# Summing layer 1's modulation on VectorE inside the value-table stage, instead of on GpSimd

## The reference

```python
mod = silu(c) @ ada_w[l] + ada_b[l]            # ada_w[l]: 1024 x 6144
sh1, sc1, g1, sh2, sc2, g2 = split(mod, 6)     # shifts, scales, gates of the layer
...
a = einsum('td,thkd->thk', tc, u_tab[ec])      # first expert table, 16384 x 1024
w = gate * gelu(a)
y = einsum('thk,thkd->td', w, v_tab[ec])       # second expert table, 16384 x 1024
```

## Time and profile before

| | |
|---|---|
| median of 3 runs | 2510.07 us (2504.06 to 2512.12) |
| the profiled execution: time | 2507.17 us |
| its span, first to last instruction | 2505.2 us |
| mean granted TensorE clock | 0.943 |
| PE matmul busy | 2200.2 us (88%) |
| DVE busy | 1557.7 us (62%) |
| ACT busy | 1188.2 us (47%) |
| POOL busy | 1122.4 us (45%) |
| DMA, mean over the span | 151 GB/s |

### The profile page before, as it was taken

The page is one execution under the profiler, slowest core; times in us unless marked ns, Lnnn a source line. Parts: engine busy times, 40 slices in busy tenths (PEclk is TensorE's granted clock), DMA queues, the critical chain, the costliest instruction groups (busy, mean ns, idle before and its releaser), DMA issues.

```text
span 2505.2 us, 40525 instructions
## 1 busy us (share of the span) xinstructions
PE 2200.2 (88%) x13500; PEld 1974.4 (79%) x13500; DVE 1557.7 (62%) x2323; ACT 1188.2 (47%) x2096; POOL 1122.4 (45%) x472
## 2 busy tenths in 40 slices
PE   5897789999997588988998968799999965999998
PEld 4786679999997567767776857799999955788886
DVE  7578338994003978888975862599900069555555
ACT  8521434555545753433442232445555467455553
POOL 0003036988887545556550300578888865000000
PEclk9698789999998999999998987899999989999999
DMA  7632033555553025665563311345555510455553
GB/s 261 223 110 84 37 136 136 181 183 185 179 182 126 0 89 199 226 209 216 211 224 129 127 59 59 130 155 178 184 184 184 177 58 0 141 193 193 193 193 109
DMA packets 103453, 378.55 MB, mean 151 GB/s; under 512 B 11488, under 2 KB 11872, under 8 KB 102880
## 3 DMA queue, kind: packets, MB, share of 16 engines
q1 hardware_dynamic: 102672, 373.74, 42.9%
q10 hardware_dynamic: 720, 4.00, 0.4%
HBM read 375.46 MB, written 2.23 MB: 151 GB/s over the span
## 4 chain that ended last, share of the span: by engine, by line
PE 33%; issue 24%; POOL 24%; DVE 12%; DMA 3%; ACT 2%; POOLq 1%; DVEq 0%; SPq 0%; ACTq 0%
PE bank L1586 21%; POOL split_lo L472 19%; PE bank L1564 3%; PE bank L1286 3%; POOL hots L483 3%; DMA ring<-stream 2%; PE bank L1249 1%; POOL ada_acc L499 1%; DVE hots L1142 1%; DVE w_lo L1175 1%; POOL ada_ring L497 1%; DMA ada_ring<-stream 1%; DVE split_lo L1174 1%; DVE hots L1140 1%; PE bank L1460 1%
## 5 line engine op out<-in xcount | busy, mean ns | idle before, releaser
L472 POOL TENSOR_TENSOR split_lo<-ring,split_hi 128x1024 fp32r<-128x1024 f32 x296 | 728.7, 2486 | 247.2 <-ACT split_hi L689 246.9
L1497 PE MATMUL bank<-h_hi,split_hi 128*128 128x256 f32 x2304 | 657.1, 285 | 29.7 <-DVE h_lo L1084 21.3
L1499 PE MATMUL bank<-h_hi,split_lo 128*128 128x256 f32 x2304 | 654.6, 284 | 0.0
L1498 PE MATMUL bank<-h_lo,split_hi 128*128 128x256 f32 x2304 | 654.6, 284 | 0.0
L1174 DVE TENSOR_TENSOR split_lo<-ring,split_hi 128x1024 fp32r<-128x1024 f32 x248 | 381.2, 1537 | 229.0 <-ACT w_hi L765 228.9
L1497 PEld LDWEIGHTS bank<-h_hi,split_hi 128*128 128x128 f32 x2304 | 444.6, 193 | 34.7 <-issue 18.6
L764 ACT ACTIVATE split_hi<-ring 128x1024 fp32r<-128x1024 f32 x248 | 263.2, 1061 | 428.1 <-PE bank L1586 356.2
L1498 PEld LDWEIGHTS bank<-h_lo,split_hi 128*128 128x128 f32 x2304 | 444.8, 193 | 0.0
L1499 PEld LDWEIGHTS bank<-h_hi,split_lo 128*128 128x128 f32 x2304 | 444.8, 193 | 0.0
L689 ACT ACTIVATE split_hi<-ring 128x1024 fp32r<-128x1024 f32 x296 | 298.5, 1051 | 274.0 <-PE bank L1499 273.8
L1586 PE MATMUL bank<-split_hi,w_hi 128*128 128x512 f32 x1024 | 326.0, 400 | 21.4 <-DVE w_lo L1175 21.3
(11 more groups left out here) (271 smaller groups left out, 2791.9 us busy)
## 6 DMA issues: line engine op xcount, KB each, us to landing
ring<-stream SPq DMA_DIRECT2D x658, 512.0 KB, 3.2
ada_ring<-stream SPq DMA_DIRECT2D x48, 512.0 KB, 4.7
spill<-tables ACTq DMA_DIRECT2D x1, 1152.0 KB, 4.2
tables<-spill ACTq DMA_DIRECT2D x1, 1152.0 KB, 7.2
xT<-x_in SPq DMA_DIRECT2D x1, 1024.0 KB, 10.0
s5raw<-s5w ACTq DMA_DIRECT2D x2, 512.0 KB, 5.1
y_out<-hT SPq DMA_DIRECT2D x1, 1024.0 KB, 3.9
KM<-mixc SPq DMA_DIRECT2D x1, 576.0 KB, 8.0
```

Source lines behind the costliest of these rows:

```text
L472: gp.tensor_tensor(split_lo[:, j, :], ring[:, (e0 + j) % RING, :], split_hi[:, j, :].bitcast(F32), ALU.subtract)\
L1497: mm(dst, hi, x_hi, start=start, stop=False, skip_group_check=not group)
L1498: mm(dst, hi, x_lo, start=False, stop=False, skip_group_check=not group)
L1499: return mm(dst, lo, x_hi, start=False, stop=stop, skip_group_check=not group)
```

## The change

The `ada_w` blocks of layer 1 are summed by DVE. The GpSimd loop is removed. DVE's loop over the value stage of layer 0 becomes six rounds of 20 blocks (and 8 blocks singly, of which the first four of the stage stand ahead of the loop as before), with one operation for each `ada_w` block, two turns after SP has issued its transfer. SP's turns become 0, 2, 4, 6, 9, 11, 13, 15. PE's code is the same. DVE's loop for layer 1 is the same as before.

```diff
+ADA_TURNS = (0, 2, 4, 6, 9, 11, 13, 15)
...
-                ada_turns = (0, 1, 4, 6, 8, 10, 12, 14)
                 with sp.Fori(0, ADA // KT, 1) as i:
                     for j in range(20):
                         sp.wait_ge(v_ready, i * 20 + (l * KEYS + SPLIT + j + 1))
                         fetch(i * 20 + (late + RING + j), (late + RING + j) % RING)
-                        if j in ada_turns:
-                            k = ada_turns.index(j)
+                        if j in ADA_TURNS:
+                            k = ADA_TURNS.index(j)
                             sp.wait_ge(ada_used, i * 8 + (ADA + k - 1))
...
-                    with pool.Fori(0, ADA // KT, 1) as i:
-                        for k in range(KT):
-                            pool.wait_ge(ada_filled[k % 2], i * (16 * KT // 2) + 16 * (k // 2 + 1))
-                            silu = siluc[:, k:k + 1].broadcast_to([P, BLOCK])
-                            if k == 0:
-
-                                pool.wait_ge(ada_columns, i + ADA // KT)
-                                gp.tensor_tensor(ada_acc[:, :], ada_ring[:, 0, :], silu, ALU.mult).then_inc(ada_used, 1)
-                            else:
-                                b = ada_ring[:, k % 2, :]
-                                gp.tensor_tensor(b, b, silu, ALU.mult).then_inc(ada_scaled, 1)
-                                pool.wait_ge(ada_scaled, i * (KT - 1) + k)
-                                gp.tensor_tensor(ada_acc[:, :], ada_acc[:, :], b, ALU.add).then_inc(ada_used, 1)
-                            pool.wait_ge(ada_used, i * KT + (ADA + k + 1))
...
+                def ada_step(i, k):
+
+                    dve.wait_ge(ada_filled[k % 2], i * (16 * KT // 2) + 16 * (k // 2 + 1))
+                    b = ada_ring[:, k % 2, :]
+                    if k == 0:
+                        dve.wait_ge(ada_columns, i + (l + 1) * (ADA // KT))
+                        ins = v.tensor_scalar(ada_acc[:, :], b, siluc[:, 0:1], None, ALU.mult)
+                    else:
+                        dve.wait_ge(ada_used, i * KT + ((l + 1) * ADA + k))
+                        ins = v.scalar_tensor_tensor(ada_acc[:, :], b, siluc[:, k:k + 1], ada_acc[:, :], ALU.mult, ALU.add)
+                    ins.then_inc(ada_used, 1)
+
+                if l + 1 < DEPTH:
+                    with dve.Fori(0, ADA // KT, 1) as i:
+                        for j in range(20):
+                            low(i, 20, j)
+                            if j - 2 in ADA_TURNS:
+                                ada_step(i, ADA_TURNS.index(j - 2))
+                    for j in range(120, LATE):
+                        low(0, 0, j)
+                    add_biases(l + 1, 0)
```

More of the change, by code:

```diff
@@ L380, in build @@
         spilled, mixc_in, tables_in = (sem(n) for n in ("spilled", "mixc_in", "tables_in"))
-        ada_used, ada_scaled, ada_columns = (sem(n) for n in ("ada_used", "ada_scaled", "ada_columns"))
+        ada_used, ada_columns = (sem(n) for n in ("ada_used", "ada_columns"))
         ada_filled = [sem(f"ada_filled{i}") for i in range(2)]
@@ L484, in _ @@
                                          ALU.mult).then_inc(hot_ready, 1)
-                if l + 1 < DEPTH:
-                    with pool.Fori(0, ADA // KT, 1) as i:
-                        for k in range(KT):
-                            pool.wait_ge(ada_filled[k % 2], i * (16 * KT // 2) + 16 * (k // 2 + 1))
-                            silu = siluc[:, k:k + 1].broadcast_to([P, BLOCK])
-                            if k == 0:
-                                pool.wait_ge(ada_columns, i + ADA // KT)
-                                gp.tensor_tensor(ada_acc[:, :], ada_ring[:, 0, :], silu, ALU.mult).then_inc(ada_used, 1)
-                            else:
-                                b = ada_ring[:, k % 2, :]
-                                gp.tensor_tensor(b, b, silu, ALU.mult).then_inc(ada_scaled, 1)
-                                pool.wait_ge(ada_scaled, i * (KT - 1) + k)
-                                gp.tensor_tensor(ada_acc[:, :], ada_acc[:, :], b, ALU.add).then_inc(ada_used, 1)
-                            pool.wait_ge(ada_used, i * KT + (ADA + k + 1))
         def out_rows(act, l, n, take):
@@ L1168, in _, with low @@
                     v.tensor_tensor(w_lo[:, j, :], grid[:, j * T:j * T + T], w_hi[:, j, :].bitcast(F32), ALU.subtract).then_inc(v_ready, 1)
-                def lows():
+                def low(i, n, j):
+                    s = j % SPLIT
+                    dve.wait_ge(vhi_ready, i * n + (l * KEYS + SPLIT + j + 1))
+                    v.tensor_tensor(split_lo[:, s, :], ring[:, (late + j) % RING, :], split_hi[:, s, :].bitcast(F32), ALU.subtract)
+                    v.tensor_tensor(w_lo[:, s, :], grid[:, bass.ds(i * (n * T) + (SPLIT + j) * T, T)],
+                                    w_hi[:, s, :].bitcast(F32), ALU.subtract).then_inc(v_ready, 1)
@@ L1172, in lows @@
                         for j in range(SPLIT):
[L1173 to L1176, removed]
@@ L1178, in _ @@
-                lows()
-                if l + 1 < DEPTH:
-                    add_biases(l + 1, 0)
+                            low(i, SPLIT, j)
                 dve.wait_ge(v_used, (l + 1) * KEYS)
```

## The result

The changed kernel takes 2430.2 us (median of 4 runs, 2428.77 to 2431.78); the kernel before took 2509.32 us in the runs beside it. The ratio is 0.9686, with a 95% interval of 0.9673 to 0.9700.

A forecast was written before the change was run, and what follows sets the result against it. The modulation in layer 0's value stage was taken as the bound: 348.2 + 19.2 = 367.4 us against 432.8, 65.4 less, so 2441.8 us, plus 2.9 to the median: 2444.7 us, range 2435 to 2466.

The forecast's parts named there:

- What bounds the kernel: Layer 0's value stage takes 432.8 us against layer 1's 348.2, losing 84.6 us to the modulation.
- What the change removes: Layer 0's value stage: 90 GpSimd operations (224.6 us), DVE's excess of 158 us and PE's wait for DVE go.
- What it adds on DVE: Layer 0's value stage: one operation of 0.75 us and seven of 1.28 a round, 58 us in all, hidden.
- the lead: DVE has w_lo ready 5.1 us before PE comes to that table block, which hides the additions.
- The waits it adds: DVE's waits for transfers before its steps: about 0.1 us at the median, up to 1.8, within its lead over PE.
- The rival of late transfers: Landings of 6.5 us in dense turns make each round's last step some 2.8 us late: 2461 us, chance 0.17.
- the end of a round: After each round's table blocks: 2.1 us sums, 0.3 wait and handover, 0.8 clock; 3.2 us a round, 19.2 in six.
- The low end, 2.2 us a round: Lowest cost given for the sums after each round's table blocks, 13 us over six rounds.
- the rival "slower": DVE's in-order wait passes transfer latency to table blocks; a landing of 10 us gives 2547 us, chance 0.04.
- DVE's excess from transfers: Rival: transfers, not GpSimd, slow DVE in layer 0's value stage, so only 35 us go: 2475 us, chance 0.04.
- The clock: Rival: the clock falls at every round's end, the high end of the sums' cost: 2463 us, chance 0.06.
- DVE's longer loop: Rival: DVE stalls once a round fetching instructions at its loop return; at 10 us each, 2475 us, chance 0.02.

The follow-up runs named there:

- two other kernels: The changed kernel with one of a round's eight column sums kept, 2423.97 us, and the changed kernel with each round's sums done twice, 2451.63 us.
- three turns of lag: The changed kernel with each of DVE's steps three turns, not two, behind the issue of its transfer: 2444.15 us, ratio 0.9745.
- the kernel with GpSimd beside it: The changed kernel with 16 GpSimd operations a round added on memory of their own, waited for by nobody: 2547.43 us, ratio 1.0176.
- a lag of one: The changed kernel with each of DVE's steps one turn, not two, behind the issue of its transfer: 2557.81 us, ratio 1.0217.
- the old turns: The changed kernel with SP's turns of the kernel before (0, 1, 4, 6, 8, 10, 12, 14): 2429.44 us, ratio 0.9704.
- the even turns: The changed kernel with turns 0, 2, 4, 6, 8, 10, 12, 14, each step two turns later: 2427.62 us, ratio 0.9685.
- fourfold sums: The changed kernel with each round's sums done four times (64 one-column instructions): 2497.22 us (median of 10), ratio 0.9952.

## Why the prediction was wrong

**What bounds the kernel** was right: the 84.6 us between the two stages were the whole matter. 73.5 of them went.

**What the change removes** was right in mechanism and size. L1174 fell from 1849 to 1224 ns and L1175 from 1069 to 418 ns, the full excess of 158 us. GpSimd brings 140 us of it back when it is only put beside the changed kernel.

**What it adds on DVE** was right: 1.28 and 0.75 us, hidden by the lead. A round took 40.3 us of DVE's time in the window shown, against the 40.9 worked out.

**The waits it adds** were right in their order and smaller than feared. Landing is 4.2 us at the median, 5.5 at most. The last step of round three ended at 1075.75 and the sums began at 1076.77: the margin of 1.0 us as worked out. The rival of late transfers occurred in single rounds of two other kernels (6.88 and 7.16 us to landing), not in six.

**The step that failed is the end of a round**, 3.2 us in the prediction and 1.85 us in the trace (56.25 - 54.4). All three of its parts were too high. The sums were put at 2.12 us "at full clock", and that row was misread. They followed an idle gap there, and the clock fell while they ran: they lasted until 1045.02 us, and the window from 1044 to 1045 has 0.76, so the fall lies near 1044.5 and not at 1044.8. Sums behind a gap at a clock of 1.00 take 1.94 us, as the first ones with three turns of lag; the other 0.18 us I put down to the lower clock. In the changed kernel they follow on table matmuls, and their weights begin to load while the last of these still run:

```profile
1076.31 0.62 PE L1591 MATMUL bank<-split_hi,w_lo 128*128 128x512 f32 x2
1076.77 1.84 PE L1254 MATMUL bank<-K,ada_acc 128*128 128x1 f32 x16
1078.47 0.72 PE L1591 MATMUL bank<-split_hi,w_hi 128*128 128x512 f32 x2
...
1076.54 1.98 PEld L1254 LDWEIGHTS bank<-K,ada_acc 128*128 128x128 f32 x16
```

From 1076.77 to 1078.47 it is 1.7 us. A row of the trace before had this price, and I passed over it. At the kernel's start 20 such instructions run in 2 us at full clock, 0.10 us each:

```profile
100.00:102.00 2.00, 2.00 (x20) 2.00 (x20) 1.40 (x2) 2.00 (x6) 0.00 (x0) 1.00 1.05 379
```

In place of 0.3 us for a wait and the handover and 0.8 us for the clock, 0.15 us are left: no wait at the sums, and the clock was 1.00 throughout. In all 6 x 1.35 = 8.1 us too much: 19.2 us against 11.1. The low end, 2.2 us a round, was itself above the truth, because its floor was the same row.

**The rest** of the miss is no step of the kernel. By its own sum the prediction came to 2441.8 us against the profiled execution; 8.1 us less is 2433.7, and the profiled execution of after took 2430.1. Of the remaining 3.6 us the spans show 3.4 outside the stage, 1.3 us ahead of it and 2.1 behind, in stages that have the same instructions; the second execution of the changed kernel starts its stage at 907.5 us and not at 910.0, so parts of this size vary between executions. I also added 2.9 us to come from the profiled execution to the median of three runs, which for a kernel with this scatter was no information. Below the low end of its terms, 2438 us, the range left only 3 us for such scatter. A slip in the rival "slower" changes nothing: by its relation a landing of 10 us gives 74.9 us a round, not 74.7.

**The rivals.** DVE's excess from transfers is refuted by the kernel with GpSimd beside it. The clock never fell behind a round. DVE's longer loop costs PE nothing: every round has the same 56.25 us. "Slower" needs a landing of over 8.7 us with a lag of two turns by its own relation, and the longest was 5.5 us; with a lag of one the kernel is slower at once.

## What to carry to other kernels

When work moves to an engine that feeds the bottleneck in order, its busy total says little. Work out the lead, the place of each step in the queue against the landing of its data, and the margin of the last step before a barrier: here a lag of two turns was right, three cost 14 us and one 128 us. Take an engine's slowdown by its neighbour as a cost of the neighbour's work: GpSimd's additions, wanted by nobody, cost 117 us. And price a short piece of work from a row in which it has the neighbours that it will have, since the same 16 instructions took 1.7, 1.9 or 3.6 us: behind table matmuls, behind a gap, at half clock.

## What the runs showed of the hardware

TensorE's clock fell to its lower level with PE busy all the time. With 16 one-column instructions between dense stretches (1.7 us) it stayed at 1.00 in every round of four profiles (the changed kernel twice, the old turns, the even turns). With 32 (3.5 us) it stayed in the five rounds without a wait ahead of them. With 64 it fell to 0.50 in every round, between 2.1 and 3.6 us into them (the windows above show the second round), with no idle time before. What decides the moment is not shown.

With a gap of 1.6 us ahead of the sums, one program took 2442 to 2444 us at a mean granted clock of 0.955 to 0.957, and 2459 us at 0.947. I hadn't expected that the scatter of a kernel's times may be its clock. The runs on record bear it out as far as a mean can: over the 29 runs of the kernel before, which has a gap in each round, longer times go with a lower mean clock (2498 us at 0.949, 2514 us at 0.944; correlation -0.74), and over the ten with fourfold sums still more so (2486 us at 0.948, 2505 us at 0.939; -0.97). No experiment separates the clock from other causes.
